# Attention scores of two heads at a time: the products with the keys' low half on 64 rows each, in the upper and in the lower half of the array

## The chip, the core and the metric

The kernel runs on one core of one Trainium2 chip. The metric is the device time of the program in microseconds (us). The core has a matrix engine (TensorE, in the profile PE for products and PEld for weight loads), three engines for elementwise work (VectorE or DVE, ScalarE or ACT, GpSimd or POOL) and SyncE (SP), which issues the transfers. Each engine runs its own instructions in the order in which they are written, and waits on semaphores for the others.

## What is computed

Two layers over 16 meta tokens and 512 real ones, with width 2048. Each layer normalises, projects, runs three kinds of heads and projects back. Only the attention heads matter here:

```python
proj = xn @ w_in                       # 16 query heads, 2 key/value heads, 64 wide
qh = rope(rms_norm(qb), pos); kh = rope(rms_norm(kb), pos)
# query block of 128, keys: 16 meta, the previous block, the block itself
s = einsum('bnqkgd,bnskd->bnkgqs', qb, k_all) * (DH_B ** -0.5)
s = where(allowed, s, NEG_INF)
mx = maximum(max(s), sink); pr = exp(s - mx)
w = pr / (sum(pr) + exp(sink - mx));  o = w @ v_all
h = h + concat(ya*silu(ga), yb*silu(gb), yc*silu(gc)) @ w_out
```

## The kernel before

**Numbers as sums of two.** TensorE reads a shorter form of a 32-bit number (fp32r). The kernel therefore splits each factor in a high and a low half and adds up products: for the two projections high x high, low x high, high x low. That is three passes of 16 steps ("ticks") for each chunk of 128 output columns, each pass cut in two products of 264 columns (one of 512 in most chunks of layer 1). `L1143` is the line of these products. A layer has 38 input chunks and 16 output chunks. Everything else on TensorE is put in between, at given chunks and ticks, by tables of lags at the head of the file. No engine reorders its work.

**Attention.** It runs in chunks 11 and later of each layer. A batch is (b, j, kv): query block b, four heads, one key head. There are 20 batches in layer 0 (block 0 holds the 16 meta tokens) and 16 in layer 1, in the order b = 1, 2, 3, 4, 0. A head of a batch is a cell. A table (`CELL_TICKS`) puts the cells 1 to 2.15 ticks apart. All the steps of a head stand at fixed lags in cells: scores 0, exponential 2 (ACT), transposes of the probabilities 4, of the meta part 7, values 9, output 10.

**Scores of a head** (`scores`, L949). A head's queries are 64 rows. `a_q_stack` holds 128 rows for each head: the queries' high half in rows 64 kv to 64 kv + 63, the low half in the other 64 rows. `a_k_hi` and `a_k_lo` hold the keys' halves, each copied into both halves of the rows. Two products with the same 128 x 128 weights, one with `a_k_hi` and one with `a_k_lo` as the moving operand, give the sum of all four half products in one PSUM bank of `ps_mix`. Heads take banks 0 and 1 in turn, and the scores of head J wait until the scores of head J - 2 have been taken out (`s_amx`).

**Taking out.** DVE's `att_mask_max` (L1429) adds the mask, takes the largest value and writes `a_p` to SBUF, one head for each cell, in the cell's own tick; a small second instruction reads the accumulated maximum. It counts `s_amx` up.

**The stack.** Four cells ahead of the first head, ACT writes the high halves for two batches (L791, 64 x 512 each), and one tick later DVE writes the low halves (L1737, 64 x 512 each).

**Other matmuls with few rows.** The recurrent heads have some: in `hgrn_increments` (L1073) the first block of layer 1 has 16 rows of keys (the meta tokens); in `hgrn_out` (L1088) the last 16 tokens of layer 0 give a product on 16 rows. In both, each fp32 product stands as two MATMULs in the trace.

## Time and profile before

| | |
|---|---|
| median of 3 runs | 1548.7 us (1548.65 to 1549.63) |
| the profiled execution | 1548.68 us, span 1546.9 us |
| TensorE busy | 1537.5 us, 99% of the span |
| DVE, ACT, POOL busy | 948.8, 646.3, 197.2 us |
| DMA | 151.78 MB, 98 GB/s on average |
| attention of layer 0, 145 to 305 us | PE 158.8, DVE 121.9, ACT 101.9, POOL 87.6 us of 160 |
| attention of layer 1, 925 to 1072 us | PE 146.5, DVE 107.9, ACT 90.5, POOL 79.6 us of 147 |

The profile counts the time of one execution from its first to its last instruction. Since matmuls are pipelined, the duration of one (0.28 us for 264 columns) is longer than the distance at which they follow one another; the distance between starts is what TensorE pays. A row "x2" holds two instructions, and the next row's start minus its own is the time of both.

### The profile page before, as it was taken

Reading aid. Unit: us, or ns where it says so; the run is one execution under the profiler, and the core shown is the slowest. Engines: PE = TensorE matmul, PEld = TensorE weight load, DVE = VectorE, ACT = ScalarE, POOL = GpSimd, SP = SyncE. Lnnn points to the kernel's source line nnn. Section 1 sums busy time; section 2 is a strip of 40 time slices with the busy share of each in tenths; the row PEclk is TensorE's granted clock in tenths of the full one; section 3 lists DMA queues with packets and bytes.
Section 4 is the critical chain, followed back from the end, with each engine's and each line's share of the span. In section 5 each row is a group of like instructions: output and inputs, shape, how many; then the busy total and the mean of one; then the engine's idle time right before and its main releaser. Section 6 shows DMA issues by size and latency. Waiting matters only on the chain.

```text
span 1546.9 us, 26360 instructions
## 1 busy us (share of the span) xinstructions
PE 1537.5 (99%) x10456; PEld 1422.7 (92%) x10456; DVE 948.8 (61%) x1829; ACT 646.3 (42%) x1290; POOL 197.2 (13%) x348
## 2 busy tenths in 40 slices
PE   8999999999999999999999999999999999999999
PEld 8999999999999999999998889888999888888888
DVE  6787788677778444343336676876777774442322
ACT  6776566622333322322336665666132343221211
POOL 0111664400000000000000016544000000000000
PEclk9999999999999999999999999999999999999999
DMA  7222111223221322443442231121223123234442
GB/s 281 100 83 82 56 56 60 73 75 97 83 84 55 107 85 97 139 150 124 133 144 86 82 109 56 56 80 58 86 79 110 56 82 109 82 135 140 142 146 69
DMA packets 39163, 151.78 MB, mean 98 GB/s; under 512 B 5360, under 2 KB 14336, under 8 KB 24064
## 3 DMA queue, kind: packets, MB, share of 16 engines
q1 hardware_dynamic: 38608, 149.52, 28.9%
q8 instruction: 83, 1.36, 0.4%
q10 hardware_dynamic: 432, 0.57, 0.1%
q14 instruction: 40, 0.33, 0.1%
HBM read 141.22 MB, written 8.59 MB: 97 GB/s over the span
## 4 chain that ended last, share of the span: by engine, by line
PE 97%; DVE 1%; ACT 1%; issue 0%; DMA 0%; POOL 0%; DVEq 0%; ACTq 0%; POOLq 0%
PE ps_gemm L1143 83%; PE ps_mix L1030 3%; PE ps_mix L949 2%; PE ps_mix L995 2%; PE ps_gemm L910 2%; PE ps_mix L963 2%; PE ps_gemm L1104 1%; PE ps_gemm L897 1%; PE ps_mix L897 1%; PE ps_mix L991 1%; PE ps_mix L1073 1%; PE ps_mix L1088 1%; PE ps_mix L1090 0%; PE ps_mix L976 0%; PE ps_mix L1047 0%
## 5 line engine op out<-in xcount | busy, mean ns | idle before, releaser
L1143 PE MATMUL ps_gemm<-x_hi,w_hi 128*128 128x264 f32 (+3 forms) x2176 | 542.3, 314 | 0.2 <-issue 0.2
L1143 PE MATMUL ps_gemm<-x_hi,w_lo 128*128 128x264 f32 (+3 forms) x2176 | 528.2, 307 | 0.0
L1143 PE MATMUL ps_gemm<-x_lo,w_hi 128*128 128x264 f32 (+3 forms) x2176 | 527.6, 307 | 0.0
L1143 PEld LDWEIGHTS ps_gemm<-x_hi,w_hi 128*128 128x128 f32 x2176 | 353.7, 189 | 19.8 <-issue 0.6
L1143 PEld LDWEIGHTS ps_gemm<-x_hi,w_lo 128*128 128x128 f32 x2176 | 352.0, 188 | 19.3
L1143 PEld LDWEIGHTS ps_gemm<-x_lo,w_hi 128*128 128x128 f32 x2176 | 351.4, 188 | 17.0
L647 ACT ACTIVATE w_hi<-w_stage 128x512 fp32r<-128x512 f32 x464 | 267.0, 618 | 169.4 <-DVE z L1307 122.7
L1215 DVE TENSOR_TENSOR w_lo<-w_stage,w_hi 128x512 fp32r<-128x512 f32 x392 | 259.1, 689 | 77.5 <-ACT w_hi L647 71.7
L1143 PE MATMUL ps_gemm<-mixed_hi,w_lo 128*128 128x264 f32 (+1 forms) x752 | 198.9, 320 | 0.0
L1143 PE MATMUL ps_gemm<-mixed_lo,w_hi 128*128 128x264 f32 (+1 forms) x752 | 198.7, 319 | 0.0
L1143 PE MATMUL ps_gemm<-mixed_hi,w_hi 128*128 128x264 f32 (+1 forms) x752 | 197.6, 318 | 0.0
L1307 DVE TENSOR_TENSOR z<-ps_gemm,res 128x528 f32<-128x528 f32 (+1 forms) x31 | 21.7, 700 | 204.3 <-PE ps_gemm L1143 204.3
L1143 PEld LDWEIGHTS ps_gemm<-mixed_hi,w_hi 128*128 128x128 f32 x752 | 124.9, 188 | 10.9
L1143 PEld LDWEIGHTS ps_gemm<-mixed_hi,w_lo 128*128 128x128 f32 x752 | 124.7, 188 | 10.2
L1143 PEld LDWEIGHTS ps_gemm<-mixed_lo,w_hi 128*128 128x128 f32 x752 | 123.9, 188 | 10.5
L614 POOL COPY tb<-z 32x528 f32<-32x528 f32 (+1 forms) x36 | 24.3, 675 | 719.2 <-DVE z L1325 521.2
L1325 DVE TENSOR_TENSOR z<-ps_gemm,rstd 128x528 f32<-128x528 f32 (+3 forms) x74 | 51.9, 701 | 101.3 <-PE ps_gemm L1143 100.1
L701 ACT ACTIVATE ta<-z 128x528 f32<-128x528 f32 (+1 forms) x40 | 25.5, 638 | 211.1 <-DVE z L1325 211.1
L546 POOL TENSOR_TENSOR w_lo<-w_stage,w_hi 128x512 fp32r<-128x512 f32 x72 | 95.9, 1333 | 1.0 <-ACT w_hi L647 1.0
L1429 DVE CUSTOM_DVE_ANT_0 a_p<-ps_mix,cst,neg_sinks 128x272 f32<-128x272 f32 (+2 forms) x144 | 63.4, 440 | 34.7 <-PE ps_mix L949 27.5
L810 ACT ACTIVATE a_p<-a_p,att_stat 128x272 f32<-128x272 f32 (+2 forms) x144 | 67.0, 466 | 15.4 <-DVE att_stat L1429 14.7
L826 ACT ACTIVATE a_pt_hi<-ps_mix 128x512 fp32r<-128x512 f32 (+1 forms) x64 | 34.9, 545 | 80.1 <-PE ps_mix L963 79.8
(194 smaller groups left out, 1626.5 us busy)
## 6 DMA issues: line engine op xcount, KB each, us to landing
w_stage<-in_w_in SPq DMA_DIRECT2D x82, 1024.0 KB, 4.9
w_stage<-in_w_out SPq DMA_DIRECT2D x32, 1024.0 KB, 5.3
res<-in_xT SPq DMA_DIRECT2D x16, 264.0 KB, 5.3
h1T<-z SPq DMA_DIRECT2D x16, 264.0 KB, 5.7
res<-h1T SPq DMA_DIRECT2D x16, 264.0 KB, 5.3
a_rden<-rden SPq DMA_DIRECT2D x32, 128.0 KB, 4.9
out<-z SPq DMA_DIRECT2D x15, 256.0 KB, 5.6
x_in<-in_xT SPq DMA_DIRECT2D x3, 1056.0 KB, 12.8
```

Source lines behind the costliest of these rows:

```text
L546: pool.tensor_tensor(wl[:, N % 3, ks], wst[:, N % 3, ks], wh[:, N % 2, ks].bitcast(F32), ALU.subtract)\
L647: act.activation(wh[:, N % 2, 4 * q:4 * q + 4], wst[:, N % 3, 4 * q:4 * q + 4], ACT.Copy)\
L810: act.activation(pr[0:nq, Q % 2, i, band(b)], pr[0:nq, Q % 2, i, band(b)], ACT.Exp, scale=-1.0, bias=st_neg[0:nq, Q % 4, i:i + 1], accum_o ...
L826: act.activation(pth[:, first:2, heads], M[:, 2].rearrange("p (s i q) -> p s i q", s=2, i=2)[:, first:2], ACT.Copy)\
L897: ins = pe.matmul(g[:, bank, 0:size], lhs, rhs[:, c:c + size], start=i == 0, stop=i == len(parts_of) - 1)
L910: ins = pe.matmul(G[:, c, bank, 0:size], ws, xs[:, k, c0:c0 + size], start=k == 0 and i == 0, stop=k == KC - 1 and i == 2)
L949: ins = pe.matmul(M[0:nq, J % 2, band(b)], qT, keys, start=k_part is kh, stop=k_part is kl)
L1030: ins = pe.matmul(o[:, :, 64 * (b % 2):64 * (b % 2) + 64], hk[:, c0 + P * b:c0 + P * b + rows], sets[:, :, 64 * b:64 * b + 64], start=True ...
L1143: ins = pe.matmul(g[:, bank, 0:size], ws, xs[:, k, c:c + size], start=tick == 0 and i == 0, stop=tick == TICKS - 1 and i == 2)
L1215: dve.tensor_tensor(wl[:, N % 3, ks], wst[:, N % 3, ks], wh[:, N % 2, ks].bitcast(F32), ALU.subtract)\
L1325: signal(dve.tensor_tensor(halves(dst, c0, w), src, halves(rstd, c0, w), ALU.mult), s_z)
L1429: signal(dve.tensor_tensor_reduce(pr[0:nq, Q % 2, i, band(b)], M[0:nq, J % 2, band(b)], mask, -DH ** -0.5, sink, ALU.add, ALU.min, st_neg[ ...
```

## The change

Per head the product of the 128-row stack with `a_k_hi` stays, and so do the sums low x high and high x high. The product with `a_k_lo` now leaves out low x low, as it takes the queries' high half alone: 64 rows. To have the two heads of a pair on different rows, the odd head's stack is turned over (low half where the even head has its high half). The two 64-row products stand one after the other behind the odd head's full one, and only then are both heads' scores announced. DVE takes out both heads in the odd head's tick. ACT writes the high half of the odd heads a second time, into the other rows; DVE makes the low halves in four instructions where there were two, and for the odd heads it writes them over the high half.

```diff
@@ ACT: the stack's high halves
+                            other = slice(64 - 64 * kv, 128 - 64 * kv)
                             act.activation(qs[MM % 2][rows, 4 * kv:4 * kv + 4, 0:nq],
                                            y[rows, 4 + 4 * j:8 + 4 * j, blk(b)], ACT.Copy).then_inc(s_qh, 1)
+                            act.activation(qs[MM % 2][other, 4 * kv + 1:4 * kv + 4:2, 0:nq],
+                                           y[rows, 5 + 4 * j:8 + 4 * j:2, blk(b)], ACT.Copy).then_inc(s_qh, 1)
@@ TensorE: scores
-                    pe.wait_ge(s_ql, 2 * MM + 2)
+                    pe.wait_ge(s_ql, 4 * MM + 4)
...
-                for k_part in (kh, kl):
-                    keys = k_part[:, kv].rearrange("p b t -> p (b t)")[:, first:first + size]
-                    ins = pe.matmul(M[0:nq, J % 2, band(b)], qT, keys, start=k_part is kh, stop=k_part is kl)
-                ins.then_inc(s_asc, 1)
+                keys, keys_lo = (a[:, kv].rearrange("p b t -> p (b t)")[:, first:first + size] for a in (kh, kl))
+                pe.matmul(M[0:nq, J % 2, band(b)], qT, keys, start=True, stop=False)
+                if i % 2:
+                    for odd in range(2):
+                        rows = slice(64 * (kv ^ odd), 64 * (kv ^ odd) + 64)
+                        q_hi = qs[MM % 2][rows, 4 * kv + i - 1 + odd, 0:nq]
+                        ins = pe.matmul(M[0:nq, odd, band(b)], q_hi, keys_lo[rows], start=False, stop=True)
+                    ins.then_inc(s_asc, 2)
@@ DVE: the stack's low halves
-                            dve.wait_ge(s_qh, 2 * MM + kv + 1)
-                            signal(dve.tensor_tensor(qs[MM % 2][other, 4 * kv:4 * kv + 4, 0:nq],
-                                                     y[rows, 4 + 4 * j:8 + 4 * j, blk(b)],
-                                                     qs[MM % 2][rows, 4 * kv:4 * kv + 4, 0:nq].bitcast(F32),
-                                                     ALU.subtract), s_ql)
+                            dve.wait_ge(s_qh, 4 * MM + 2 * kv + 2)
+                            for odd, to in ((0, other), (1, rows)):
+                                hi = qs[MM % 2][rows, 4 * kv + odd:4 * kv + 4:2, 0:nq].bitcast(F32)
+                                signal(dve.tensor_tensor(qs[MM % 2][to, 4 * kv + odd:4 * kv + 4:2, 0:nq],
+                                                         y[rows, 4 + odd + 4 * j:8 + 4 * j:2, blk(b)], hi,
+                                                         ALU.subtract), s_ql)
@@ DVE: scores taken out
-                    if at:
-                        att_mask_max(layer, *at)
+                    if at and at[1] % 2:
+                        att_mask_max(layer, at[0], at[1] - 1)
+                        att_mask_max(layer, at[0], at[1])
```

The wait of `att_meta_out` for the scores of its own tick is counted in pairs too; it stands in the tick of a fourth head, where the number it waits for is the one of before.

TensorE, two neighbouring heads of block 1 in layer 0 (128 x 144 is the shape of the moving keys, `a_q_stack_83` the stack). Before:

```order
L949 MATMUL ps_mix<-a_k_hi,a_q_stack_83 128x144
L949 MATMUL ps_mix<-a_k_lo,a_q_stack_83 128x144
L1143 MATMUL ps_gemm<-x_hi,w_hi 128x264 x2
L1143 MATMUL ps_gemm<-x_lo,w_hi 128x264 x2
L1143 MATMUL ps_gemm<-x_hi,w_lo 128x264 x2
L949 MATMUL ps_mix<-a_k_hi,a_q_stack_83 128x144
L949 MATMUL ps_mix<-a_k_lo,a_q_stack_83 128x144
L991 MATMUL ps_mix<-a_pmeta_t,a_vmeta 128x512
```

After, the same place:

```order
L951 MATMUL ps_mix<-a_k_hi,a_q_stack_83 128x144
L1150 MATMUL ps_gemm<-x_hi,w_hi 128x264 x2
L1150 MATMUL ps_gemm<-x_lo,w_hi 128x264 x2
L1150 MATMUL ps_gemm<-x_hi,w_lo 128x264 x2
L951 MATMUL ps_mix<-a_k_hi,a_q_stack_83 128x144
L956 MATMUL ps_mix<-a_k_lo,a_q_stack_83 128x144 x2
L998 MATMUL ps_mix<-a_pmeta_t,a_vmeta 128x512
```

The even head's second product has moved behind the odd head's first, next to the odd head's own; both of L956 have 64 rows. The number of MATMULs is the same.

DVE, the same two heads and the stack of the next batches (`L1429`, after `L1436`, takes scores out). Before:

```order
L1429 ISA a_p,att_stat<-ps_mix,cst,neg_sinks 128x144
L1429 ISA att_stat 128x1
L1384 TENSOR_TENSOR ta<-tb,cst 128x16
L1385 TENSOR_TENSOR ta<-ta,z 128x16
L1386 SCALAR_TENSOR_TENSOR ta<-tb,z 128x512
L1737 TENSOR_TENSOR a_q_stack_82<-y,a_q_stack_82 64x512 x2
L1429 ISA a_p,att_stat<-ps_mix,cst,neg_sinks 128x144
L1429 ISA att_stat 128x1
```

After:

```order
L1391 TENSOR_TENSOR ta<-tb,cst 128x16
L1392 TENSOR_TENSOR ta<-ta,z 128x16
L1393 SCALAR_TENSOR_TENSOR ta<-tb,z 128x512
L1746 TENSOR_TENSOR a_q_stack_82<-y,a_q_stack_82 64x2x128 x4
L1436 ISA a_p,att_stat<-ps_mix,cst,neg_sinks 128x144
L1436 ISA att_stat 128x1
L1436 ISA a_p,att_stat<-ps_mix,cst,neg_sinks 128x144
L1436 ISA att_stat 128x1
```

The even head's scores are now taken out behind the pooling steps and the stack, not ahead of them.

## Rows read from the trace of the kernel before

**Rows 1.** The page: TensorE's busy share, and its granted clock in 40 slices.

```profile
PE 1537.5 (99%) x10456; PEld 1422.7 (92%) x10456; DVE 948.8 (61%) x1829; ACT 646.3 (42%) x1290; POOL 197.2 (13%) x348
...
PEclk9999999999999999999999999999999999999999
```

**Rows 2.** The waits of PE: line, releaser, us in total, times, longest.

```profile
PE ps_mix L949 <- DVE att_stat L1429: 0.4, 1, 0.4
```

**Rows 3.** Groups by shape, PE: rows*columns of the weights, moving operand, count.

```profile
L949 PE MATMUL ps_mix<-a_k_hi,a_q_stack 128*128 128x272 f32 x96 | 29.6, 309 | 0.0
...
L949 PE MATMUL ps_mix<-a_k_hi,a_q_stack 128*128 128x144 f32 x32 | 8.2, 255 | 0.0
...
L949 PE MATMUL ps_mix<-a_k_hi,a_q_stack 128*16 128x16 f32 x16 | 2.9, 179 | 0.4 <-DVE att_stat L1429 0.4
```

**Rows 4.** Timeline of PE, one head's scores: start, us, operation.

```profile
203.39 0.41 PE L1143 MATMUL ps_gemm<-x_hi,w_lo 128*128 128x264 f32 x2
203.63 0.28 PE L949 MATMUL ps_mix<-a_k_hi,a_q_stack 128*128 128x272 f32 x1
203.75 0.29 PE L949 MATMUL ps_mix<-a_k_lo,a_q_stack 128*128 128x272 f32 x1
203.88 0.41 PE L1143 MATMUL ps_gemm<-x_hi,w_hi 128*128 128x264 f32 x2
```

**Rows 5.** Timeline of PE, L1073 in layer 0: all on 128 rows.

```profile
347.86 0.41 PE L1143 MATMUL ps_gemm<-x_hi,w_lo 128*128 128x264 f32 x2
348.10 1.05 PE L1073 MATMUL ps_mix<-h_v,h_kn 128*128 128x128 f32 x8
...
349.24 0.41 PE L1143 MATMUL ps_gemm<-x_lo,w_hi 128*128 128x264 f32 x2
```

**Rows 6.** Timeline of PE, L1073 in layer 1: the first two on 16 rows.

```profile
1117.31 0.39 PE L1143 MATMUL ps_gemm<-x_lo,w_hi 128*128 128x512 f32 x1
1117.54 0.40 PE L1143 MATMUL ps_gemm<-x_hi,w_lo 128*128 128x512 f32 x1
1117.86 1.35 PE L1073 MATMUL ps_mix<-h_v,h_kn 16*128 16x128 f32 x8
...
1119.28 0.39 PE L1143 MATMUL ps_gemm<-x_lo,w_hi 128*128 128x512 f32 x1
```

**Rows 7.** Timeline of PEld, the same place: in brackets the idle time ahead.

```profile
1117.86 1.16 PEld L1073 LDWEIGHTS ps_mix<-h_v,h_kn 16*128 16x128 f32 x8 [0.36 <-issue]
```

**Rows 8.** Timeline of PE, L1088 in layer 0: two products on 16 rows.

```profile
353.04 0.39 PE L1088 MATMUL ps_mix<-h_att,h_v 128*128 128x128 f32 x2
...
353.58 0.39 PE L1088 MATMUL ps_mix<-h_att_tail,h_v 16*128 16x16 f32 x2
...
354.47 0.40 PE L1143 MATMUL ps_gemm<-x_lo,w_hi 128*128 128x264 f32 x2
```

**Rows 9.** Timelines of PE and DVE: scores and their taking out, at three places.

```profile
162.02 0.23 PE L949 MATMUL ps_mix<-a_k_hi,a_q_stack 128*128 128x144 f32 x1
...
162.03 0.37 DVE L1429 CUSTOM_DVE_ANT_0 a_p<-ps_mix,cst,neg_sinks 128x144 f32<-128x144 f32 x1
...
169.72 0.37 DVE L1429 CUSTOM_DVE_ANT_0 a_p<-ps_mix,cst,neg_sinks 128x144 f32<-128x144 f32 x1 [0.26 <-PE ps_mix L949]
...
172.79 0.23 PE L949 MATMUL ps_mix<-a_k_hi,a_q_stack 128*128 128x144 f32 x1
...
174.17 0.37 DVE L1429 CUSTOM_DVE_ANT_0 a_p<-ps_mix,cst,neg_sinks 128x144 f32<-128x144 f32 x1
...
1062.94 0.29 PE L949 MATMUL ps_mix<-a_k_hi,a_q_stack 128*128 128x272 f32 x1
...
1062.74 0.50 DVE L1429 CUSTOM_DVE_ANT_0 a_p<-ps_mix,cst,neg_sinks 128x272 f32<-128x272 f32 x1
```

**Rows 10.** The tile a_q_stack: count, min/median/max ns, first and last start, forms.

```profile
L791 ACT ACTIVATE a_q_stack<-y x36: 243/620/632, 145.8 to 1046.6; 64x512 fp32r<-64x512 f32 x32, 64x64 fp32r<-64x64 f32 x4
L1737 DVE TENSOR_TENSOR a_q_stack<-y,a_q_stack x36: 219/726/1859, 146.5 to 1047.5; 64x512 fp32r<-64x512 f32 x32, 64x64 fp32r<-64x64 f32 x4
```

More of the change, by code:

```diff
@@ L1437, in att_meta_out @@
                 if now:
-                    dve.wait_ge(s_asc, 4 * (ATT_Q0[layer] + now[0]) + now[1] + 1)
+                    dve.wait_ge(s_asc, 4 * (ATT_Q0[layer] + now[0]) + (now[1] + 1) // 2 * 2)
                 dve.wait_ge(s_amt, Q + 1)
```

## The prediction

> **What bounds the kernel now.** I read the page's busy shares and clock first. TensorE is busy for 99% of the span and has the clock of 2.4 GHz in every slice [rows 1], so the time is the sum of the distances at which its instructions follow one another, and any edit must be priced in these. Then the waits: in the place that the change touches PE waits once, for 0.4 us, for scores to be taken out [rows 2]. DVE and ACT follow TensorE and cost nothing as long as they keep up. Last the timeline, at the scores and at every place where TensorE works on fewer than 128 rows, because the change brings such products in.
>
> **What the change removes.** A head's two products take 0.12 us each from start to start [rows 4], the same as a projection's product of 264 columns (0.24 for two). There are 96 heads with 272 key columns, 32 with 144 and 16 with 16 columns [rows 3], thus 48, 16 and 8 pairs. No MATMUL goes away. Two of the four of a pair get 64 rows, and the hoped-for gain is that these two run side by side. If they did so for nothing else, a pair of 272 columns would take 3 distances and not 4: 48 x 0.12 = 5.8 us less. At 144 columns a product is already paced by its weight load (0.11 us each, below), so those gain little.
>
> **What it adds on TensorE: a change of the number of rows, twice per pair.** The trace of before has this in two places.
> - L1073 in layer 0 has eight products of 128 columns on 128 rows. From the pair of projection products ahead to the pair behind but one it takes 349.24 - 347.86 = 1.38 us [rows 5]; four projection products are 4 x 0.12 = 0.48, which leaves 0.90 for the eight, 0.11 each. In layer 1 the first two of the eight are on 16 rows. From 1117.54 to 1119.28 are 1.74 us, less two projection products of 512 columns at 0.23 (1117.31 to 1117.54) [rows 6]: 1.28 for the eight. Going to 16 rows and back cost **0.38 us**. The weight load shows where: it started 0.36 us after the last one had ended, with nothing to wait for [rows 7], while elsewhere it runs under the product ahead.
> - L1088: from 353.04 to 354.47 are 1.43 us [rows 8] for eight products at 0.11 and two of 264 columns at 0.12, 1.12 us: **0.31 us** for two of 16 columns on 16 rows, there and back.
>
> What the rows say: before products with another number of rows TensorE finishes what it has, and only then loads weights. In 64-row form no row shows it, so this is a transfer by likeness. The Trainium skill, TensorEngine Tiling (Array Packing), section Key Properties, says that changing the tiling mode, and not just the tile, drains the engine. By that rule every pair pays twice; the trace agrees for 16 rows (0.38 and 0.31 us), and it speaks against this change.
>
> Per pair of 272 columns: the 0.38 were paid with a 512-column product ahead, which streams for its whole distance as the 272-column one here does, but with 128-column products inside. The last product inside must stream out before the way back: (272 - 128) x 0.11/248 us (from 0.23 for 512 and 0.12 for 264 columns) = 0.06 more. Side by side the two halves gain 0.01, since the second's weight load (0.11) sets its start and not the 0.12. So 0.38 + 0.06 - 0.01 = +0.43: 48 x 0.43 = **20.6 us**. For 144 columns the product ahead is a short one, as in L1088; between 0.31 and 0.38 I take 0.34: 16 x 0.34 = **5.4**. For 16 columns the weights have 16 columns too and load faster; at most 0.31, I take 0.20: 8 x 0.20 = **1.6**. Sum +27.6 us.
>
> Ends of this term: if the two weight loads, for different rows, also ran side by side, 64 x 0.11 = 7 us less; if the price were that of L1088 everywhere, 64 x 0.07 = 4.5 less: +16. If the lower half also had to wait for the upper (each change of rows is half of 0.38), 64 x 0.19 = 12 more: +40. Below nothing it goes only without the drain (rival 1). The values between are nearest to L1073, which has the same kind of neighbours.
>
> **What it adds on DVE.** Taking the even head out now waits for the odd head's tick. The next pair's first scores need the even head's bank. Before, that mask had been ready a cell earlier; now it ends about where the odd head's mask ended. I compared, for all pairs, the end of the odd head's mask with the start of the next pair's scores: it is later at 13 places [rows 9] (the first at 162.03 + 0.37 against 162.02, the last at 1062.74 + 0.50 against 1062.94, with the small read behind it), by 9.0 us in all. The worst is the pair of 169.72: the odd mask starts at 174.17, behind pooling and stack, and the next scores at 172.79. There PE would wait some 1.8 us. Since DVE now takes the even head first, the end that counts is 0.58 earlier where DVE is behind: then 3.2 us in all are left. And TensorE comes 0.4 us later per pair by its own drain. Between 0 and 9 I take **+3 us**. Everywhere else the next scores start after the mask's end, so nothing is added.
>
> **What it adds on the stack.** ACT gets 36 more writes of half size. One costs between 0.24 (64 x 64) and 0.62 us (64 x 512) [rows 10], thus 9 to 22 us more of busy time on an engine at 42% [rows 1]. DVE does 72 half writes for 36, at most 0.22 each for the instruction itself: up to 8 us. Both are four cells (some 7 us) ahead of the scores, so they stay hidden; what stands behind them on ACT is the exponential and `w_hi`, both also with a cell or more in hand. If that cover were gone at the places where DVE is already late, it is in the 9 us above. I take 0.
>
> **Sum.** 27.6 + 3 = 31, on the profiled execution's 1548.68, which is also the median: **1579 us**. The time added sits between TensorE's own instructions, so no other engine can hide it.
>
> **Rivals.**
> 1. **No drain for 64 rows, and the halves overlap** (the other side). For it: 16 rows need a finer cut of the array than 64 do, and no row shows 64. The Trainium skill, TensorE: Matmul & The Clock Gate, Part 3, gives for packed matmuls a span of one matmul plus about 4 ns for each further tile. As a mechanism here: pair 0.36 and not 0.48 us, 5.8 us less. Against it: both places with 16 rows show the break. It decides if the way there and back costs below 0.12 us. With DVE's waits in between 0 and 9: 1543 us where DVE keeps up (chance 0.07), 1546 to 1552 where it takes the gain back (0.07).
> 2. **No drain, no overlap.** The halves run at 0.12 like full ones, and only DVE's waits are left: 3 to 9 us, 1552 to 1558. Chance 0.08. For it: at 144 columns weight loads set the pace anyhow.
> 3. **The halves wait for one another too.** +40 and DVE's 3: 1592 us; within the forecast's upper end. Chance 0.12, and a further 0.04 for dearer ways yet.
>
> **How the numbers follow.** The forecast, drain twice per pair, has 0.62 (1563 to 1588: +16 with nothing from DVE, less 2 for rows' rounding, up to 27.6 and 9 with 3 more). With rival 3 slower cases hold 0.78, with rival 2 0.86. 0.2% are 3.1 us, about what a measurement of this kernel can tell from no change. Faster: 0.07. Same: 0.07. Slower: 0.86. The range from 1552 to 1596 leaves out rival 1 for the most part (0.12) and what is dearer than rival 3 (0.04).
>
> **What would show it.** In the timeline of after: the weight load of the first 64-row product begins only when the product ahead has ended, 0.2 us later than its place, and that of the next 128-row work once more; from the odd head's full product to the next other product about 0.80 us, where three distances were 0.37. The group of weight loads on 64 rows, and those right behind it, show idle time ahead, put down to nothing. The clock stays in every slice. PE's waits for `att_stat` grow from 0.4 to some 3 us, the longest in chunk 12 of layer 0 near 173 us. Wrong it is if the 64-row weight loads run under the product ahead: then rival 1 or 2. If the two starts of L956 are more than 0.2 us apart, rival 3.

## The result, and the profile after

| | before | after |
|---|---|---|
| median | 1548.7 us (4 runs, 1548.6 to 1549.6) | 1580.9 us (4 runs, 1580.3 to 1585.2) |
| ratio, 95% interval | | 1.0212 [1.0199, 1.0225] |
| profiled execution, span | 1548.7, 1546.9 us | 1585.2, 1583.4 us |
| PE busy, PE idle (span less busy) | 1537.5, 9.4 us | 1562.3, 21.1 us |

The change makes the kernel 32.2 us slower; the forecast was 30 us slower (1579). The sum came out, but not its terms: they erred in opposite directions by about the same amount, and that is luck.

The page of after (busy times, the clock in 40 slices, the shares of the chain that ended last) answers to [rows 1]:

```profile
PE 1562.3 (99%) x10456; PEld 1427.2 (90%) x10456; DVE 966.7 (61%) x1865; ACT 662.8 (42%) x1326; POOL 192.2 (12%) x348
...
PEclk9999999999999999999999999999999999999999
...
PE 92%; DVE 4%; issue 1%; ACT 1%; DMA 1%; POOL 1%; SPq 0%; DVEq 0%; POOLq 0%; ACTq 0%
```

With the same 10456 products PE is busy for 25 us more, and idle for 12 us more; 4 to 5 us of the 25 are a lower clock in this one execution (see "The clock" below). Of the chain 97% was PE in before, and DVE held 1%; now DVE holds 4% of it.

The scores of one odd head in block 2, as in [rows 4], on PE and then on PEld (start, us, operation):

```profile
206.01 0.41 PE L1150 MATMUL ps_gemm<-x_hi,w_lo 128*128 128x264 f32 x2
206.26 0.29 PE L951 MATMUL ps_mix<-a_k_hi,a_q_stack 128*128 128x272 f32 x1
206.48 0.39 PE L956 MATMUL ps_mix<-a_k_lo,a_q_stack 64*128 64x272 f32 x2
206.80 0.50 PE L998 MATMUL ps_mix<-a_pmeta_t,a_vmeta 128*128 128x512 f32 x1
207.14 0.39 PE L1002 MATMUL ps_mix<-a_pt_hi,a_v 128*128 128x512 f32 x1
...
206.14 0.19 PEld L951 LDWEIGHTS ps_mix<-a_k_hi,a_q_stack 128*128 128x128 f32 x1
206.47 0.19 PEld L956 LDWEIGHTS ps_mix<-a_k_lo,a_q_stack 64*128 64x128 f32 x2
206.80 0.19 PEld L998 LDWEIGHTS ps_mix<-a_pmeta_t,a_vmeta 128*128 128x128 f32 x1
```

The weight load of the full product starts 0.12 us ahead of its product, under the one before. Those of the halves start with the halves, and so does that of the next 128-row product. From the full product to the halves are 0.22 us here, from the halves to the next product 0.32. But the row "x2" of PEld is 0.19 us long for two loads, and a single one is just as long: the two run side by side. The product behind the next one is late too: from L998 to L1002 are 0.34 us, where e1 below has 0.23.

Over the 48 pairs of 272 columns the median distances are 0.26 (full to first half), 0.003 (half to half) and 0.32 us (half to next). The sum of the three is 0.62 us by the median, and 0.54 at the place shown. The first distance depends on what stands ahead: 0.22 behind a projection product, 0.30 behind a short product with `a_pmeta`. Full rows have 0.12 and 0.21 at such places, so the way in adds 0.09 us at either.

The waits of PE in after (line, releaser, us, times, longest), where [rows 2] had 0.4 us:

```profile
PE ps_mix L951 <- DVE att_stat L1436: 7.3, 7, 2.0
PE ps_mix L951 <- DVE a_q_stack L1746: 3.0, 2, 2.5
```

And DVE's part of the stack, one row of after by tile as in [rows 10]; below it the group by shape of before and of after (busy us, mean ns of one, idle time ahead of it), each in its own fence:

```profile
L1746 DVE TENSOR_TENSOR a_q_stack<-y,a_q_stack x72: 183/422/1556, 147.1 to 1083.1; 64x256 fp32r<-64x256 f32 x64, 64x32 fp32r<-64x32 f32 x8
...
L1746 DVE TENSOR_TENSOR a_q_stack<-y,a_q_stack 64x256 fp32r<-64x256 f32 x64 | 48.1, 752 | 6.0 <-ACT a_q_stack L794 4.0
```

```profile
L1737 DVE TENSOR_TENSOR a_q_stack<-y,a_q_stack 64x512 fp32r<-64x512 f32 x32 | 31.6, 986 | 2.3 <-ACT a_q_stack L791 1.3
```

The same numbers, in twice as many instructions, take 48.1 us and not 31.6. The median of a half write is 0.42 us, the longest 1.56: it is not a price per instruction but something that some of them meet. And PE now waits for this stack, twice, where it never did.

So there are three suspects: the 64 rows, the late taking out, and the stack. My theory gave them 27.6, 3 and 0 us.

### The profile page after: what moved, and what is told of

It reads as the page before. It is cut to its first block, busy times and chain, and to the rows that moved or that the text cites. A ratio compares the mean times of both kernels' runs of the same rounds, so it can differ in the third digit from the quotient of the medians.

```text
span 1583.4 us, 26432 instructions
## 1 busy us (share of the span) xinstructions
PE 1562.3 (99%) x10456; PEld 1427.2 (90%) x10456; DVE 966.7 (61%) x1865; ACT 662.8 (42%) x1326; POOL 192.2 (12%) x348
## 4 chain that ended last, share of the span: by engine, by line
PE 92%; DVE 4%; issue 1%; ACT 1%; DMA 1%; POOL 1%; SPq 0%; DVEq 0%; POOLq 0%; ACTq 0%
PE ps_gemm L1150 78%; PE ps_mix L1037 3%; DVE a_q_stack L1746 2%; PE ps_mix L970 1%; PE ps_mix L1002 1%; PE ps_gemm L913 1%; PE ps_mix L956 1%; PE ps_mix L951 1%; PE ps_gemm L900 1%; PE ps_gemm L1111 1%; PE ps_mix L998 1%; DMA x_in<-in_xT 1%; PE ps_mix L900 1%; PE ps_mix L1080 1%; PE ps_mix L1095 1%
## 5 line engine op out<-in xcount | busy, mean ns | idle before, releaser
L1150 PEld LDWEIGHTS ps_gemm<-mixed_hi,w_hi 128*128 128x128 f32 x752 | 125.0, 188 | 10.9
L1150 PEld LDWEIGHTS ps_gemm<-mixed_hi,w_lo 128*128 128x128 f32 x752 | 124.7, 188 | 10.3
L1150 PEld LDWEIGHTS ps_gemm<-mixed_lo,w_hi 128*128 128x128 f32 x752 | 124.0, 188 | 10.4
L1436 DVE CUSTOM_DVE_ANT_0 a_p<-ps_mix,cst,neg_sinks 128x272 f32<-128x272 f32 (+2 forms) x144 | 63.4, 441 | 31.9 <-PE ps_mix L956 25.2
```

Of the source, the lines that this page charges most:

```text
L1150: ins = pe.matmul(g[:, bank, 0:size], ws, xs[:, k, c:c + size], start=tick == 0 and i == 0, stop=tick == TICKS - 1 and i == 2)
L1436: signal(dve.tensor_tensor_reduce(pr[0:nq, Q % 2, i, band(b)], M[0:nq, J % 2, band(b)], mask, -DH ** -0.5, sink, ALU.add, ALU.min, st_neg[ ...
```

## The experiments

All ratios are against the kernel before, run beside them (its median was 1549.1, 1549.1 and 1548.8 us in the three sessions: e1 to e4, e5 to e8, e9 to e11).

| | taken from | median us | ratio, 95% interval | PE busy, idle |
|---|---|---|---|---|
| e1 pairs, full rows | after | 1573.3 | 1.0160 [1.0143, 1.0177] | 1544.1, 27.3 |
| e2 halves, same rows | after | 1577.3 | 1.0182 [1.0167, 1.0197] | 1561.9, 13.3 |
| e3 single heads | before | 1594.6 | 1.0293 [1.0278, 1.0309] | 1584.3, 8.3 |
| e4 stack a cell later | after | 1579.6 | 1.0195 [1.0179, 1.0210] | 1559.0, 19.2 |
| e5 pairs, old stack | before | 1560.1 | 1.0072 [1.0057, 1.0087] | 1540.8, 16.7 |
| e6 turned stack | before | 1560.5 | 1.0075 [1.0060, 1.0090] | 1540.2, 18.5 |
| e7 split only | before | 1559.9 | 1.0071 [1.0054, 1.0088] | 1540.8, 17.5 |
| e8 eight halves | e5 | 1560.8 | 1.0076 [1.0061, 1.0092] | 1539.1, 19.4 |
| e9 = e7, light GpSimd | e7 | 1548.8 | 1.0000 [0.9990, 1.0009] | 1537.1, 10.3 |
| e10 = e1, light GpSimd | e1 | 1562.1 | 1.0084 [1.0067, 1.0101] | 1541.5, 18.7 |
| e11 = after, light GpSimd | after | 1573.2 | 1.0156 [1.0141, 1.0171] | 1555.5, 15.3 |

### e1: the same pairs, all products on 128 rows

```diff
-                        q_hi = qs[MM % 2][rows, 4 * kv + i - 1 + odd, 0:nq]
-                        ins = pe.matmul(M[0:nq, odd, band(b)], q_hi, keys_lo[rows], start=False, stop=True)
+                        q_hi = qs[MM % 2][:, 4 * kv + i - 1 + odd, 0:nq]
+                        ins = pe.matmul(M[0:nq, odd, band(b)], q_hi, keys_lo, start=False, stop=True)
```

> The changed kernel with one thing undone: the two products with the keys' low half use all 128 rows again (the low x low part is back, the result is the full one). Pairs, turned stack and taking out by pairs stay. Theory 1 (two causes: the way to 64 rows and back costs TensorE 0.25 us a pair of 272 columns with the two halves fully side by side, some 16 us in all; the rest is DVE taking scores out late, with the clock falls behind it): 1565 us, range 1561 to 1568, PE's waits for att_stat and a_q_stack still 8 us or more. Rival (the loss is what the prediction's sum says, 27.6 us for the change of rows and 3 for DVE): 1553 us, waits of 3 us.

Measured 1573.3 us, +24.2: far above both. Without any 64-row product three quarters of the loss are still there. Its odd head at the same place:

```profile
204.77 0.29 PE L951 MATMUL ps_mix<-a_k_hi,a_q_stack 128*128 128x272 f32 x1
204.90 0.41 PE L956 MATMUL ps_mix<-a_k_lo,a_q_stack 128*128 128x272 f32 x2
205.15 0.39 PE L998 MATMUL ps_mix<-a_pmeta_t,a_vmeta 128*128 128x512 f32 x1
205.38 0.40 PE L1002 MATMUL ps_mix<-a_pt_hi,a_v 128*128 128x512 f32 x1
...
PE ps_mix L951 <- DVE att_stat L1436: 12.1, 13, 2.3
```

The breaks around the products are gone (0.38 us for three), but PE waits longer for DVE than in after: 12.1 us against 7.3. TensorE is no longer held up by its own products, so it meets DVE sooner. What the 64 rows cost on TensorE is therefore hidden in part. After less e1 is PE busy +18.2 us and idle -6.2. The clock of after's profiled execution holds 4 to 5 of the 18.2, which leaves about 14.

### e2: both halves on the same 64 rows, stack of before

```diff
-                        rows = slice(64 * (kv ^ odd), 64 * (kv ^ odd) + 64)
+                        rows = slice(64 * kv, 64 * kv + 64)
```

with ACT's second write away, and DVE's low halves in two instructions as before.

> The changed kernel, but both heads' 64-row products on the same half of the rows (the stack is the one of before, no second write by ACT and no split write by DVE). Theory 1 (in the changed kernel the two run side by side): the second starts 0.11 to 0.12 us behind the first and not 0.003, so 48 x 0.12 + 16 x 0.11 + 8 x 0.02 = 7.7 us more than the changed kernel on TensorE, less what the simpler stack gives back on DVE (up to 3): 1584 to 1589 us. Rival (different rows gain nothing, or only the start stamps are close): no slower than the changed kernel, 1577 to 1581 us.

Measured 1577.3 us, 3.6 less than after and below the 1584 to 1589 that TensorE's side had. Yet on TensorE these halves are dearer than those of after, not cheaper:

```profile
209.08 0.37 PE L949 MATMUL ps_mix<-a_k_hi,a_q_stack 128*128 128x272 f32 x1
209.38 0.51 PE L954 MATMUL ps_mix<-a_k_lo,a_q_stack 64*128 64x272 f32 x2
209.83 0.66 PE L968 MATMUL ps_mix<-cst,a_p 128*128 128x128 f32 x4
```

From the full product to the next other one are 0.75 us; by the median of the 48 pairs it is 0.74, against 0.62 in after. The halves do run one behind the other, 0.23 us apart by the median, where two full products are 0.125 apart. Why they are further apart than full ones no run shows. TensorE loses by it: PE busy against e5, which has the same stack and pairs, is +21.1 us, where the turned rows cost 14 (e11 less e10, below). The edit took away the turned stack as well, and that gave back more than the rows took. I had changed two things at once, and this pointed to the stack.

### e3: one 64-row product for each head, in before

```diff
+                    if k_part is kl:
+                        rows = slice(64 * kv, 64 * kv + 64)
+                        qT, keys = qs[MM % 2][rows, 4 * kv + i, 0:nq], keys[rows]
```

> The kernel before with one part of the change alone: each head's product with the keys' low half uses 64 rows (queries' high half; low x low is left out, as in the changed kernel), in the head's own tick; stack and taking out are those of before. So there are 144 changes of rows and back, with nothing side by side and nothing moved on DVE. Theory 1 (0.26 us to 64 rows and 0.32 back, against 0.24 for both products at 272 columns; 0.47 against 0.22 at 144; 0.15 against 0.05 at 16): 96 x 0.34 + 32 x 0.24 + 16 x 0.1 = 42 us, 1591 us, range 1586 to 1596, PE's waits on DVE about 0. The prediction's price (0.44, 0.35, 0.20 per head): 96 x 0.44 + 32 x 0.35 + 16 x 0.20 = 57 us, 1606 us. If the change of rows were cheap and DVE the whole cause: below 1555 us.

Measured 1594.6 us, +45.5 for 144 trips to 64 rows and back: 0.32 us each. There are no pairs, no late taking out and no new stack in it, and PE never waits for DVE in the attention's scores. PE's idle time even fell by 1.1 us, so this is the clean price. The run lies in the range that was expected of it.

```profile
209.94 0.37 PE L952 MATMUL ps_mix<-a_k_hi,a_q_stack 128*128 128x272 f32 x1
210.24 0.39 PE L952 MATMUL ps_mix<-a_k_lo,a_q_stack 64*128 64x272 f32 x1
210.56 0.66 PE L966 MATMUL ps_mix<-cst,a_p 128*128 128x128 f32 x4
210.97 0.49 PE L1146 MATMUL ps_gemm<-x_hi,w_hi 128*128 128x264 f32 x2
```

The same head in before:

```profile
201.39 0.37 PE L949 MATMUL ps_mix<-a_k_hi,a_q_stack 128*128 128x272 f32 x1
201.60 0.29 PE L949 MATMUL ps_mix<-a_k_lo,a_q_stack 128*128 128x272 f32 x1
201.73 0.60 PE L963 MATMUL ps_mix<-cst,a_p 128*128 128x128 f32 x4
202.08 0.49 PE L1143 MATMUL ps_gemm<-x_hi,w_hi 128*128 128x264 f32 x2
```

0.30 in and 0.32 out, where it was 0.21 and 0.13. The four products behind take 0.41 us and not 0.35, so the way back is felt by the second product behind it too. Set head by head against before, the medians at 272 columns are 0.09 us more in, 0.19 more out and 0.10 more from the next product to the one behind it (0.06 where the next one has 128 columns). In all a trip costs 0.38 us at 272 columns, 0.30 at 144 and 0.18 at 16. Over the 144 heads this adds up to 46.3 us, nearly all of the 46.8 that PE is busy for longer.

### e4: DVE's stack one cell later

```diff
-                    m = att_pair_at(layer, n, tick, 1)
+                    m = att_pair_at(layer, n, tick, 2)
```

> The changed kernel, but DVE writes the stack's low halves one cell later, in the tick of a third head, which takes no scores out, and not ahead of the pair in the second head's tick. TensorE's instructions are the same. Theory 1 (a good third to a half of the loss is DVE's lateness): PE's waits fall from 11 us to 4 or less, the granted clock stays up, 1567 to 1573 us. Rival (DVE costs 3 us only): 1578 to 1581 us.

Measured 1579.6 us (1577.0 to 1580.7), 1.3 less than after, and far from 1567 to 1573. The rival held. PE's waits moved:

```profile
PE ps_mix L970 <- DVE a_pt_lo L1468: 3.5, 7, 1.9
PE ps_mix L951 <- DVE a_q_stack L1746: 3.0, 2, 2.5
PE ps_mix L951 <- DVE att_stat L1436: 2.3, 3, 0.8
```

`att_stat` fell from 7.3 to 2.3 us, and in its place the low halves of the transposed probabilities (`a_pt_lo`) rose to 3.5. What DVE is late with changed, and not that it is late: to move the stack by a cell is no cure. A part of the gain seems to have gone to the clock: the execution of 1577.0 us had a mean clock of 1.000, 3.2 us below the fastest of after (1580.3, also 1.000), and the other three had 0.996 to 0.998.

### e5 and e6: pairs alone, and the turned stack alone

e5 is before with the scores and the taking out in pairs, all products on 128 rows, and the stack of before:

```diff
+                pe.matmul(M[0:nq, J % 2, band(b)], qT, keys, start=True, stop=False)
+                if i % 2:
+                    for odd in range(2):
+                        q_hi = qs[MM % 2][:, 4 * kv + i - 1 + odd, 0:nq]
+                        ins = pe.matmul(M[0:nq, odd, band(b)], q_hi, keys_lo, start=False, stop=True)
+                    ins.then_inc(s_asc, 2)
...
+                    if at and at[1] % 2:
+                        att_mask_max(layer, at[0], at[1] - 1)
+                        att_mask_max(layer, at[0], at[1])
```

> Pairs alone: two heads' products with the low half behind the odd head's full one and both taken out in the odd head's tick, as in the changed kernel, but all on 128 rows and with the stack of before (the result is the full one, low x low included). It differs from the first experiment (pairs, full rows, turned stack: +24 us) in the stack alone. Theory A (the late taking out and the split stack each cost something, and the stack is the larger part, since the experiment with 64-row halves on the same rows and the stack of before came to +28.6, of which some 23 are TensorE's own): 1554 to 1560 us. Rival B (pairing is the whole cost, the stack is hidden as the prediction said): 1570 to 1574 us.

e6 is before with nothing but the change's writes of ACT and DVE into the stack (each head still takes its own two products on 128 rows, and the sum over the rows does not depend on their order):

```diff
+                            act.activation(qs[MM % 2][other, 4 * kv + 1:4 * kv + 4:2, 0:nq],
+                                           y[rows, 5 + 4 * j:8 + 4 * j:2, blk(b)], ACT.Copy).then_inc(s_qh, 1)
...
+                            for odd, to in ((0, other), (1, rows)):
+                                hi = qs[MM % 2][rows, 4 * kv + odd:4 * kv + 4:2, 0:nq].bitcast(F32)
+                                signal(dve.tensor_tensor(qs[MM % 2][to, 4 * kv + odd:4 * kv + 4:2, 0:nq],
```

> The stack alone: the kernel before with the turned stack (ACT's second write of the odd heads, DVE's four half writes where there were two); scores, products and taking out are those of before, all on 128 rows. Theory A: DVE's writes of the stack go from 34 us to some 51 us of busy time as in the changed kernel, and PE waits 3 us for a_q_stack at the start of the two attention stages: 1553 to 1562 us. Rival B (hidden, four cells ahead of use): 1548 to 1551 us.

e5 measured 1560.1 us, +11.0, at the upper edge of what was expected; e6 1560.5, +11.5, within it. Neither has a 64-row product. Together they are 22.5 of e1's 24.2 us. The 1.7 that are left may be their interplay, but each ratio's interval is over 2 us wide to either side. So the late taking out costs 11 us, not 3, and the stack 11 us, not 0. The place in e5 that the prediction called the worst:

```profile
173.26 2.53 DVE L1742 TENSOR_TENSOR a_q_stack<-y,a_q_stack 64x512 fp32r<-64x512 f32 x2
175.83 0.37 DVE L1434 CUSTOM_DVE_ANT_0 a_p<-ps_mix,cst,neg_sinks 128x144 f32<-128x144 f32 x1
176.24 0.37 DVE L1434 CUSTOM_DVE_ANT_0 a_p<-ps_mix,cst,neg_sinks 128x144 f32<-128x144 f32 x1
...
176.26 0.33 PE L949 MATMUL ps_mix<-a_k_hi,a_q_stack 128*128 128x144 f32 x1 [1.94 <-DVE att_stat L1434]
```

The forecast's 1.8 us are here 1.94, even with the stack of before. But the waits for `att_stat` in e5 are 5.0 us of 11.0. Others came with them: `a_pmeta` 0.7, `issue` (a pause that the profile puts down to nothing) 1.6 where there were 0.2, `a_pt_lo` 1.2 where there were 1.0. PE's idle time is up by 7.3 us, and its busy time by 3.3 for the same products. That last part stands in e6 (+2.7) and e7 (+3.3) too. A part of it comes with the waits. Product by product against before, the projection products behind a wait of e5 slip by 0.12 to 0.16 us more than the idle time ahead of them (2.10 for a wait of 1.94, 0.93 for 0.78). e5 has 19 idle stretches of over 0.1 us and before has 10, so that is some 1.3 of the 3.3 us (an estimate); what the rest is stays open.

### e7: the split alone

DVE's two instructions become four, written to the same places as before; ACT has no second write.

```diff
-                            signal(dve.tensor_tensor(qs[MM % 2][other, 4 * kv:4 * kv + 4, 0:nq],
...
+                            for odd in range(2):
+                                hi = qs[MM % 2][rows, 4 * kv + odd:4 * kv + 4:2, 0:nq].bitcast(F32)
+                                signal(dve.tensor_tensor(qs[MM % 2][other, 4 * kv + odd:4 * kv + 4:2, 0:nq],
```

> Less still: the kernel before, and DVE writes the stack's low halves in four instructions of 64 x 256 in place of two of 64 x 512, to the same places; ACT writes nothing more. If the number of DVE instructions next to GpSimd's work is what makes the stack dear (one of 64 x 256 takes 0.42 us by the median and 0.75 on average, up to 1.56), DVE's busy time for them is 48 us or more and the run is within 2 us of the turned stack's. If ACT's second write is what delays: 1549 to 1550 us.

Measured 1559.9 us, +10.9, as contention has it: the split alone is 10.9 of the stack's 11.5, and the 0.6 between them are within the noise. The start of the attention of layer 1 in e7, on POOL, DVE and PE:

```profile
932.64 4.30 POOL L546 TENSOR_TENSOR w_lo<-w_stage,w_hi 128x512 fp32r<-128x512 f32 x3
...
932.24 4.98 DVE L1739 TENSOR_TENSOR a_q_stack<-y,a_q_stack 64x256 fp32r<-64x256 f32 x4 [0.77 <-ACT a_q_stack L791]
...
937.27 0.33 PE L949 MATMUL ps_mix<-a_k_hi,a_q_stack 128*128 128x144 f32 x1 [2.22 <-DVE a_q_stack L1739]
```

In after, the same place:

```profile
942.76 1.29 POOL L546 TENSOR_TENSOR w_lo<-w_stage,w_hi 128x512 fp32r<-128x512 f32 x1
942.80 4.81 DVE L1746 TENSOR_TENSOR a_q_stack<-y,a_q_stack 64x256 fp32r<-64x256 f32 x4 [1.21 <-ACT a_q_stack L794]
944.53 2.80 POOL L546 TENSOR_TENSOR w_lo<-w_stage,w_hi 128x512 fp32r<-128x512 f32 x2 [0.47 <-ACT w_hi L647]
...
947.66 0.49 PE L951 MATMUL ps_mix<-a_k_hi,a_q_stack 128*128 128x144 f32 x1 [2.49 <-DVE a_q_stack L1746]
```

And in before:

```profile
926.14 2.70 DVE L1737 TENSOR_TENSOR a_q_stack<-y,a_q_stack 64x512 fp32r<-64x512 f32 x2 [0.77 <-ACT a_q_stack L791]
```

Four halves take 4.98 us where two wholes took 2.70, while GpSimd makes `w_lo` of the next weights by subtractions of 1.3 to 1.4 us each (4.30 for three). Each DVE instruction seems to wait for GpSimd's anew. That four are ready 2.1 to 2.3 us later is what PE waits for here. This is only one part of the price: of PE's 8.1 us more of idle time in e7, the waits for `a_q_stack` are 2.7. The waits for `a_pt_lo`, which DVE makes too, come to 3.3 where there were 1.0, and pauses that the profile puts down to nothing (`issue`) ahead of the projection products to 2.0 where there were 0.2. The "four cells ahead" of the prediction do not hold at the start of a layer's attention, where the first stack is wanted as soon as it is made.

### e8: eight halves in one trip

e5, with the low-key products left out of the first three pairs of every eight heads, and eight 64-row products behind the last one's full product (which thus stand for all eight). The scores of most heads lack that term, so this measures TensorE's time and not the result.

```diff
+                if i == 3 and kv:
+                    for h in range(8):
+                        two, rows = h % 2, slice(64 * (h % 2), 64 * (h % 2) + 64)
+                        lo = kl[rows, two].rearrange("p b t -> p (b t)")[:, first:first + size]
+                        ins = pe.matmul(M[0:nq, two, band(b)], qs[MM % 2][rows, 4 * two + h // 2, 0:nq], lo,
+                                        start=False, stop=h > 5)
```

> The price of going to 64 rows and back, by another number of products per trip. As the pairs with full rows and the stack of before, but the products with the keys' low half are left out of the first three pairs of each eight heads, and eight products on 64 rows (queries' high half, in turn in the upper and in the lower half of the rows) stand behind the eighth head's full one. Their sums go to the wrong heads, so the output is wrong; the work on TensorE is what is measured. By the starts seen so far (0.26 us to 64 rows, 0.003 between two halves, 0.32 back at 272 columns) a trip takes 0.58 + 3 x 0.12 = 0.94 us for eight halves, against 8 x 0.127 = 1.02 for eight full products and the way on: at or just below the pairs with full rows, -2 to +1 us. By the prediction's price (0.43 and more for each trip over what it holds, halves 0.11 apart): 12 x 0.4 us slower, +5 us.

```profile
215.19 0.37 PE L949 MATMUL ps_mix<-a_k_hi,a_q_stack 128*128 128x272 f32 x1
215.49 0.76 PE L954 MATMUL ps_mix<-a_k_lo,a_q_stack 64*128 64x272 f32 x8
216.18 0.66 PE L970 MATMUL ps_mix<-cst,a_p 128*128 128x128 f32 x4
```

Measured 1560.8 us, +0.7 on e5 and within its interval. The trip with eight halves takes 0.99 us (215.19 to 216.18; the median of the twelve with 272 columns is 1.00). Full products would take 0.21 + 8 x 0.126 = 1.22 (0.21 is the first distance behind a product with `a_pmeta`, as in before at 201.39). The second product behind the trip is late by 0.06, which leaves 0.16 less. PE's busy time is 1.7 us below e5's, and DVE's waits take it back (`att_stat` 6.7 against 5.0). So the overlap that the change wants exists, but it takes many halves in one trip to pay for the way there and back: a trip with two costs 0.22 us more than full products (e11 against e10, below), one with eight 0.16 less, so the line between the two crosses zero at five to six (an estimate from these two). The two PSUM banks of the scores hold two heads.

### e9: the split with a lighter GpSimd

e7 with GpSimd's subtractions replaced by writes of zero. The products low x high of the projections thus add nothing: the work on TensorE is the same, the numbers are not.

```diff
-                pool.tensor_tensor(wl[:, N % 3, ks], wst[:, N % 3, ks], wh[:, N % 2, ks].bitcast(F32), ALU.subtract)\
-                    .then_inc(s_wlp, 1)
+                pool.memset(wl[:, N % 3, ks].bitcast(F32), 0.0).then_inc(s_wlp, 1)
```

> The kernel before with the stack's low halves in four DVE instructions (measured at +10.9 us), and GpSimd's share of the weights' low halves (72 subtractions of 128 x 512 from SBUF, 1.3 us each, in chunks 12 to 20) left out: GpSimd writes zeros there, which reads nothing and takes less time. So part of the projections' sum is missing. Theory A (a DVE instruction waits while a GpSimd one with two inputs runs, and more instructions wait more often): DVE's busy time for the stack falls from 50 to 25 to 32 us, 1548 to 1552 us. Rival (four instructions are dear in themselves, or by the semaphore between them): busy time stays above 40 us, 1556 to 1560 us.

Measured 1548.8 us, ratio 1.0000 [0.9990, 1.0009]: the split costs nothing now. Groups of e7, then of e9:

```profile
L1739 DVE TENSOR_TENSOR a_q_stack<-y,a_q_stack 64x256 fp32r<-64x256 f32 x64 | 46.8, 730 | 3.4 <-ACT a_q_stack L791 1.3
...
L546 POOL TENSOR_TENSOR w_lo<-w_stage,w_hi 128x512 fp32r<-128x512 f32 x72 | 94.9, 1320 | 0.9 <-ACT w_hi L647 0.9
```

```profile
L1738 DVE TENSOR_TENSOR a_q_stack<-y,a_q_stack 64x256 fp32r<-64x256 f32 x64 | 32.6, 509 | 3.4 <-ACT a_q_stack L790 1.3
...
L546 POOL MEMSET w_lo<- 128x512 f32 x72 | 37.9, 526 | 1.4 <-ACT w_hi L646 1.4
```

The same 64 instructions take 32.6 us in place of 46.8 when GpSimd writes only. There is no run of the unsplit stack beside plain writes, so a small gain of the lighter GpSimd itself could hide in this zero. By an estimate it is below 2 us: in before PE was idle for 1.7 us in the two attention stages. GpSimd is also busy for a shorter time, so this run does not part "reads nothing" from "is there less". The Trainium skill, SBUF — State Buffer, section "Who interferes with whom", says that a DVE instruction with two SBUF inputs contends with a GpSimd instruction that reads SBUF, not with one that only writes it. That fits both rows (730 ns against 509).

### e10 and e11: full and half rows with a lighter GpSimd

The same edit in e1 and in after.

> The changed kernel with full rows (measured at +24.2 us), and GpSimd's subtractions left out in the same way (zeros are written). Theory A: the stack's part of 11.5 us goes, and the part of the late taking out shrinks as DVE has less to catch up: 1550 to 1558 us, PE's waits for att_stat 5 us or less. Rival: 1570 us or more.

> The changed kernel whole, with 64-row halves, and GpSimd's subtractions left out in the same way. Against the run with full rows beside it this gives what the 64 rows cost when DVE is hardly late. Theory A (a trip to 64 rows costs what the single heads show, 45.5/144 = 0.32 us, and the halves side by side give back 48 x 0.127 + 16 x 0.11 = 7.9 us; in the changed kernel half of it was hidden because TensorE would have waited for DVE anyway): 72 x 0.32 - 7.9 = 15 us more than its neighbour, 12 to 17. Rival (the 64 rows cost 8 us, as the changed kernel against its full-row form shows): 6 to 9 us more.

e10 measured 1562.1 us, +13.3, above the 1550 to 1558 that were expected. It lost the stack's part (11.2 less than e1), but the pairs' part stayed, so it needs no slow GpSimd. Its largest wait:

```profile
PE ps_mix L950 <- DVE att_stat L1435: 8.1, 10, 1.9
```

and that of e11:

```profile
PE ps_mix L950 <- DVE att_stat L1435: 5.7, 6, 1.7
```

e11 measured 1573.2, +11.1 on e10, between the two expectations. By the pages PE is busy for 14.0 us more (1555.5 against 1541.5) and idle for 3.4 us less (15.3 against 18.7). So **14 us is what 72 trips to 64 rows cost TensorE**, with the overlap of the halves already taken off. Pair by pair the two traces say the same. At 272 columns the medians are 0.09 us more in, 0.12 less for the second half, 0.19 more out and 0.06 more behind: 0.22 a pair. At 144 columns a pair costs 0.18, at 16 columns 0.15. Summed over all pairs these are 10.4 + 2.9 + 1.0 = 14.3 us. And 3.4 us of it (6.2 in after against e1, where DVE is later still) is time in which TensorE would have waited for DVE anyway.

## Why the prediction was right, and where its terms were not

| term | forecast | measured |
|---|---|---|
| 64 rows | 27.6 (16 to 40) | 14 on TensorE; 7.6 on the end (after less e1) |
| late taking out | 3 (0 to 9) | 11.0 (e5) |
| stack | 0 | 11.5 (e6), of which the split 10.9 (e7) |
| left over (e1 less e5 and e6) | | 1.7 |
| sum | 31 | 31.8; 32.2 measured, against another session's before |

**TensorE bounds: right. That its edits' prices add up: only in part.** PE is busy for 98 to 99% of the span in all runs. But 14 us of its own work came to 7.6 at the end, since the rest lay where it would have waited for DVE.

**The break at a change of rows: right in mechanism, too dear.** The signs came as named: late weight loads, and a break both ways. L951, which is full, is not slower; the break is at L956 and behind it. But the named 0.80 us from full to next product were 0.54 to 0.62. The step that failed is "the second's weight load (0.11) sets its start": the halves start 0.003 us apart, and their weight loads run together too. That takes 0.12 us off a pair of 272 columns where I took off 0.01. This was the lower end of my term (7 us less), which I had no row for. The other step is the trip's own price in a pair: 0.34 us (0.09 in, 0.19 out, 0.06 behind) and not 0.38 + 0.06. The 0.06 that I added for longer products were not there. For single heads the likeness was good: e3 has 0.38, 0.30 and 0.18 us for 272, 144 and 16 columns, and the rows of before had 0.38 (L1073) and 0.31 (L1088). By columns the term was 20.6 + 5.4 + 1.6 and is 10.4 + 2.9 + 1.0. The Trainium skill, TensorEngine Tiling (Array Packing), section Key Properties, was right that changing the mode drains the array, and TensorE: Matmul & The Clock Gate, Part 3, right that a further packed tile takes about 4 ns (3 measured). I had treated them as rivals, and they hold together.

**"The time added sits between TensorE's own instructions, so no other engine can hide it": wrong.** It holds only while no other wait stands behind. Once DVE was late, a slower TensorE waited less for it.

**Late taking out: right place, wrong size.** The worst wait is where it was said (2.0 us, chunk 12 of layer 0). The step that failed was to count only the next pair's scores. A mask that comes a cell later also makes the steps behind it on DVE late, and these give PE waits of their own. The waits for these scores alone came to 5.0 us in e5, between the 3.2 and the 9.0 of my count; the other 6 of its 11.0 us are the later steps' waits and PE's longer busy time, for which I had no term.

**The stack hidden: wrong.** Two steps failed. I priced a half write by the instruction's fixed cost (0.22 us) with a whole one's spread in sight: 219 to 1859 ns in [rows 10], median 726. That spread was the sign that something else holds these instructions up. And I let a lead of four cells stand for all batches; the first of each layer has none.

**The clock: mostly right.** In the profiled execution it fell in three short stretches (columns: window, us, busy us and count of PE, PEld, DVE, ACT, POOL, granted clock, DMA share, GB/s):

```profile
178.00:182.00 4.00, 3.79 (x16) 3.38 (x17) 1.72 (x6) 1.60 (x5) 0.00 (x0) 0.64 0.01 4
946.50:953.50 7.00, 5.84 (x26) 5.58 (x27) 2.61 (x8) 1.23 (x4) 0.83 (x1) 0.55 0.00 1
963.50:967.50 4.00, 3.48 (x17) 3.35 (x17) 1.23 (x6) 0.92 (x4) 0.00 (x0) 0.59 0.03 10
```

In each of them the products go at 1.2 GHz for a part of the window. Each fall comes late in a wait of PE for DVE or within 1 us behind it: waits of 1.99 us ahead of 178.21, 2.49 ahead of 947.66 and 1.74 ahead of 964.02. This execution took 1585.2 us, the others 1580.3 to 1581.0 at a mean clock of 0.999 to 1.0. So 4 to 5 us of the profiled span came with the lower clock, and the median holds none of them. With them off, PE's busy rise of 24.8 us is about 20.

**The rivals.** No drain (1 and 2) fell by the timeline. Halves that wait for one another (3) fell too: they start together. Slower was right at 0.86.

## What to carry to other kernels

Keep a trip between row shapes for blocks of many products: one way there and back cost 0.3 to 0.4 us here at 144 and 272 columns, against 0.12 us that each second overlapping half saves. Count the products behind the trip as well: the second one was still late. An engine that "keeps up" is not free to be changed: price the split of an instruction by the median and the longest of its like in the trace, not by its shortest, and look for the place at which its lead is zero. And when a sum comes out, take its terms apart all the same: here one was 20 us too high and two others together 20 too low, and the near hit was luck.

## What the runs showed of the hardware that was not expected

- Weight loads for different 64-row halves run side by side: two in 0.19 us, as one alone, and the products 0.003 us apart. On the same rows (e2) the products are 0.23 us apart, further than two full ones (0.125).
- A trip to 64 rows and back cost 0.38 us at 272 columns, 0.30 at 144 and 0.18 at 16 (e3). It has three parts: 0.09 in, 0.19 out and 0.06 to 0.10 at the second product behind (272 columns). With two halves in it, a trip costs 0.22 us more than full products; with eight (e8) it is paid back with 0.16 us to spare.
- Splitting a DVE subtraction of two SBUF operands in two raised its busy time from 31.6 to 46.8 us beside GpSimd's subtractions, but only to 32.6 beside GpSimd's plain writes.
- Stretches at 1.2 GHz came with PE's waits of 1.7 to 2.5 us in the profiled execution of after, and, once or twice each, with waits of 1.9 to 2.5 us in those of e4, e6, e7 and e8 (granted clock 0.57 to 0.66 in the 4 to 5 us behind). e1 has as long waits (2.3 and 2.5 us) and a mean clock of 1.000 in its profiled execution: the same wait does not always bring it on.
